# Prompt attention: the second head's probabilities divided on GpSimd between its masks, in place of ScalarE

## What is computed

```python
def fox_block(q, k, v, cq, ck, qpos, kpos):
    s = jnp.einsum('bqhd,bkhd->bhqk', q, k).astype(jnp.float32) * (HEAD_DIM ** -0.5)
    bias = jnp.swapaxes(cq, 1, 2)[..., :, None] - jnp.swapaxes(ck, 1, 2)[..., None, :]
    mask = kpos[None, :] <= qpos[:, None]
    p = jax.nn.softmax(jnp.where(mask, s + bias, -jnp.inf), axis=-1)
    return jnp.einsum('bhqk,bkhd->bqhd', p.astype(v.dtype), v)
```

## Time and profile before

| What | Value |
| --- | --- |
| time, median of 3 runs | 2518.85 us (2517.77 to 2520.33) |
| span of the profiled execution, first to last instruction | 2515.4 us |
| PE busy | 2438.8 us, 97% |
| DVE busy | 1502.0 us, 60% |
| ACT busy | 1078.2 us, 43% |
| POOL busy | 138.5 us, 6% |
| prompt attention | from 652.4 to 695.9 us of the span |
| PE busy in 665.50 to 675.32 us | 8.68 of 9.82 us |

### The profile page before, as it was taken

The page is one execution under the profiler, slowest core; times in us unless marked ns, Lnnn a source line. Parts: engine busy times, 40 slices in busy tenths (PEclk is TensorE's granted clock), DMA queues, the critical chain, the costliest instruction groups (busy, mean ns, idle before and its releaser), DMA issues. The chain is left out here.

```text
span 2515.4 us, 46249 instructions
## 1 busy us (share of the span) xinstructions
PE 2438.8 (97%) x18529; PEld 2219.3 (88%) x18529; DVE 1502.0 (60%) x2111; ACT 1078.2 (43%) x1873; POOL 138.5 (6%) x150
## 2 busy tenths in 40 slices
PE   8999999999988989999999999999999999999998
PEld 7998998899667877998999899899989779988997
DVE  7754764423546866873675687267462478735754
ACT  5542543322645654452353445245352444523542
POOL 0000001000203421000000100000010010000001
PEclk9999999999999999999999999999999999999999
DMA  4222324222480004322223332223423132322332
GB/s 134 84 86 74 84 65 152 60 75 62 151 267 20 4 13 142 85 75 88 80 84 124 119 84 75 96 73 90 136 75 97 63 102 84 92 80 75 90 105 104
DMA packets 285466, 229.41 MB, mean 91 GB/s; under 512 B 24924, under 2 KB 237046, under 8 KB 285320
## 3 DMA queue, kind: packets, MB, share of 16 engines
q1 hardware_dynamic: 285320, 227.38, 30.0%
HBM read 212.43 MB, written 14.91 MB: 90 GB/s over the span
## 5 line engine op out<-in xcount | busy, mean ns | idle before, releaser
L544 PE MATMUL ps<-row_hi,hid_hi 128*128 128x512 f32 x880 | 345.5, 393 | 0.0
L544 PE MATMUL ps<-row_hi,hid_lo 128*128 128x512 f32 x880 | 344.6, 392 | 0.0
L544 PE MATMUL ps<-row_lo,hid_hi 128*128 128x512 f32 x880 | 344.4, 391 | 0.0
L485 DVE TENSOR_TENSOR row_lo<-row_raw,row_hi 128x512 fp32r<-128x512 f32 x200 | 143.5, 731 | 265.9 <-ACT row_hi L477 265.7
L477 ACT ACTIVATE row_hi<-row_raw 128x512 fp32r<-128x512 f32 x200 | 124.1, 629 | 406.6 <-DMA row_raw<-in_ffn_w_out_dram 217.5
L544 PEld LDWEIGHTS ps<-row_lo,hid_hi 128*128 128x128 f32 x880 | 165.2, 188 | 36.9
L544 PEld LDWEIGHTS ps<-row_hi,hid_hi 128*128 128x128 f32 x880 | 165.1, 188 | 36.1
L544 PEld LDWEIGHTS ps<-row_hi,hid_lo 128*128 128x128 f32 x880 | 165.1, 188 | 36.0
L736 PE MATMUL ps<-t_hi,pair_hi 128*128 128x320 f32 x608 | 188.2, 310 | 3.0 <-DVE hid L1017 3.0
L736 PE MATMUL ps<-act_lo,pair_hi 128*128 128x320 f32 x608 | 187.9, 309 | 0.0
L736 PE MATMUL ps<-t_lo,pair_hi 128*128 128x320 f32 x608 | 187.9, 309 | 0.0
(11 more groups left out here) (453 smaller groups left out, 5688.9 us busy)
## 6 DMA issues: line engine op xcount, KB each, us to landing
pair_raw<-in_ffn_w_in_dram SPq DMA_DIRECT2D x104, 512.0 KB, 5.1
row_raw<-in_ffn_w_out_dram SPq DMA_DIRECT2D x160, 256.0 KB, 2.9
ring_raw<-in_ffn_w_in_dram SPq DMA_DIRECT2D x72, 512.0 KB, 5.2
pair_raw<-in_even_w_in_dram SPq DMA_DIRECT2D x22, 512.0 KB, 3.8
x_memory<-x SPq DMA_DIRECT2D x15, 512.0 KB, 2.6
x<-x_memory SPq DMA_DIRECT2D x15, 512.0 KB, 4.2
norm_buf<-in_norm_g_dram SPq DMA_DIRECT2D x12, 512.0 KB, 5.4
x<-in_x_prompt_dram SPq DMA_DIRECT2D x8, 512.0 KB, 4.9
```

Of the source, the lines that this page charges most:

```text
L485: dve.tensor_tensor(row_lo[n][:, :], raw, row_hi[n][:, :].bitcast(F32), ALU.subtract).then_inc(s_row_lo, 1)
L544: mm = pe.matmul(ps[:, bank, :], a[:, k, t * P:(t + 1) * P], w[n][:, :], start=(k == 0 and w is row_hi and a is left_hi), stop=(k == kt - ...
```

## The change

The second head's division leaves ACT. POOL does it with a `tensor_scalar` by the same column of reciprocals, in place on the same rows, behind the same wait for `s_rs`, and sets the same semaphore `s_np`. POOL does masks 0 and 1 first, and then by turns the division of step n and the mask of step n+2. Nothing else is changed. Later lines move: the file of the changed kernel has one line more behind this place, and ACT's lines in between have lower numbers.

```diff
@@ -1546,14 +1546,7 @@
                                    bias=nmax[:, b + h:b + h + 1], scale=-1.0,
                                    accum_out=esum[:, b + h:b + h + 1]).then_inc(s_ex, 1)
 
-            def normalised(n):
-                p, qt, kl, b = pstep(n)
-                act.wait_ge(s_rs, n + 1)
-                act.activation(prob[n % 2][1][:, 0:kl], prob[n % 2][1][:, 0:kl], ACT.Copy,
-                               scale=rsum[:, b + 1:b + 2]).then_inc(s_np, 1)
-
             exponentials(0)
-            normalised(0)
             exponentials(1)
             for n in range(PSTEPS + 1):
                 if n < PSTEPS:
@@ -1562,8 +1555,6 @@
                     if n >= 2:
                         act.wait_ge(s_o, n - 1)
                     act.activation(prob_t[n % 2][0][:, 0:kl], ps[:, 4, 0:kl], ACT.Copy).then_inc(s_pta, 1)
-                if n + 1 < PSTEPS:
-                    normalised(n + 1)
                 if n >= 1:
                     p, qt, kl, b = pstep(n - 1)
                     act.wait_ge(s_o, n)
@@ -1637,10 +1628,20 @@
                 pool.tensor_tensor(block, block, causal.rearrange("p (o c) -> p o c", o=1).broadcast_to([P, 2, P]),
                                    ALU.add).then_inc(s_mask, 1)
 
+            def normalised(n):
+                p, qt, kl, b = pstep(n)
+                pool.wait_ge(s_rs, n + 1)
+                pool.tensor_scalar(prob[n % 2][1][:, 0:kl], prob[n % 2][1][:, 0:kl], rsum[:, b + 1:b + 2], None, ALU.mult)\
+                    .then_inc(s_np, 1)
+
             pool.wait_ge(s_att_const, 16)
             pool.wait_ge(s_cr, 16 * 4)
+            mask(0)
+            mask(1)
             for n in range(PSTEPS):
-                mask(n)
+                normalised(n)
+                if n + 2 < PSTEPS:
+                    mask(n + 2)
             pool.wait_ge(s_fall, 16 * NSEQ)
             pool.tensor_copy(f_twice[:, :, 64:128], f_all).then_inc(s_f_twice, 1)
```

## The result

The change makes the kernel slower. The time after is 2531.09 us, the median of four runs (2528.63 to 2533.63), beside 2519.59 us for four runs of the kernel before. The ratio is 1.0043, with a 95% interval of 1.0031 to 1.0054: 11 us where 1.4 were forecast, and outside the range. The profiled run took 2528.63 us.

A forecast was written before the change was run, and what follows sets the result against it. A chain of waits through exponentials, DVE and PE was taken as the bound, not ACT. Late second heads, 4 x (0.20 + 0.16) = 1.4 us, gave 2518.85 + 1.4 = 2520.3 us; the range was 2517.0 to 2526.0 us.

The forecast's parts named there:

- What is added: 16 divisions on POOL, 0.78 us at 512 keys and 0.63 at 384, making PE's second-head transposes 0.20 and 0.16 us late.
- The formula around it: POOL's division ends at DVE's division end plus its own duration less 0.14 us; PE starts 0.05 us later.
- D: Duration of POOL's second-head division, put at 0.78 us at 512 keys and 0.63 at 384.
- r: Start of DVE's reciprocal in a step, from which the prediction counts the times of DVE, POOL and PE.
- sign of being wrong: The prediction would be wrong above all if DVE's division lengthened or POOL's duration fell outside 0.6 to 1.3 us.
- At 256 columns free: PE wants the second head at r + 1.66; POOL's result is ready by r + 1.19 at the latest, costing nothing.
- ACT's removal: Taking 16 divisions, 8.9 us in all, off ACT gains nothing, since DVE's division and biased scores take longer.
- The masks' place: Masks behind POOL's divisions cost nothing; DVE's 256-column division falls from 0.62 to 0.35 us, which gains nothing.
- Biased scores don't collide with POOL: DVE's biased scores, with one input in PSUM, run beside POOL's division; taken as free.
- Rival 2: DVE first, but POOL's division slower than its two-input product: over 5.0 us slower, near 2526 us, chance 0.07.
- Rival 1: POOL goes first and DVE's division ends only after POOL's: 5.2 us slower, 2524.0 us, chance 0.2.
- Rivals 3 and 4: Biased scores wait for POOL, 5.3 us slower, chance 0.04; exponentials earlier close PE's gaps, at most 4.6 us gained, chance 0.04.

## Why the prediction was wrong

**The step that failed is "What is added": POOL's division costed at 0.78 us at 512 keys and 0.63 at 384.** It is 1.56 and 1.24 us alone. I had placed it between the copy and the two-input product because it has one input like the copy. The runs show that inputs don't set it: the same division as a product of two inputs takes 1.04 us, with one input 1.56. The rows of the trace thus were no bounds. The formula around it was exact: with D = 1.56, POOL ends at r + 0.69 + 1.56 - 0.14 = r + 2.11, PE starts at r + 2.16, and r + 2.17 was measured; at 384 with 1.24, r + 1.77, and so it was. Put into the prediction's own sum, the measured durations give 4 x (0.98 + 0.77) = 7.0 us where it had 1.4. The prediction had named a POOL duration outside 0.6 to 1.3 us as its sign of being wrong, and so it came. The Trainium skill, "GPSIMD Engine Reference", section 3.1, gives 1.03 cycles per element for such a body. By this an estimate for 384 more columns is 0.33 us; the trace doesn't agree, at 1564 - 602 ns = 0.96 us, three times as much.

**"At 256 columns free" held in three groups of four.** The due time r + 1.66 counted on the next group's scores, which the last group doesn't have. There the short steps cost 0.85 us. With it the sum is 7.9 us, against 7.7 measured.

**What held.** DVE goes first and keeps its 0.49 and 0.42 us. Its 256-key division fell to 0.35 us (354 ns). ACT's removal gained nothing that the runs show: without its short divisions a middle group was still 9.82 and 9.80 us, and with all of them gone a group grew by 1.70 us for 1.76 us of lateness. The masks' place costs nothing. Biased scores don't collide with POOL: 0.55 us each with POOL's division running at 681.65 and 682.13. The last POOL copy kept nobody.

**The rivals.** Rival 2, POOL slower than its two-input product, is what happened, with a chance of 0.07 and a time near 2526 us; its size was open upwards and I gave it almost none. Rival 1, POOL first, didn't occur in the change, but it did in all sixteen steps with the product of two inputs, and in one step with the constant factor. Rivals 3 and 4 didn't occur.

**The total** has a second part that the prediction left out: the lower clock. It was 0.9924 on average against 0.9950, and what brought it there is not shown.

## What to carry to other kernels

A duration on GpSimd isn't to be interpolated between other operations: one form can cost 1.5 times another that does more. Before work is moved to an engine that looks idle, compare the time that its result has with the operation's whole duration there, and measure that first. Here, by the prediction's own terms, only a division of up to 0.58 us would have been in time at 512 keys (1.18 - 0.05 + 0.14 - 0.69), and it takes 1.56. An engine's free time counts only where the result has time to wait, as in the short steps, and the last round of a loop, which has no next round's work as a cover, has to be costed by itself.

## What the runs showed of the hardware

- `tensor_scalar` on GpSimd, f32, 128 partitions, with nothing beside it: 1.56, 1.24, 0.92 and 0.60 us at 512, 384, 256 and 128 columns. `tensor_tensor` with the factor broadcast: 1.04, 0.83, 0.61 and 0.40 us, while it holds DVE up.
- What decides who goes first is open; the start in the trace doesn't tell it. Against DVE's `tensor_scalar`, which started 0.05 to 0.07 us earlier, GpSimd's `tensor_scalar` by the column of factors came second in every step of the change. Its `tensor_tensor` with the factor broadcast, 0.04 to 0.05 us behind DVE, came first in all 16 steps. But the `tensor_tensor` that multiplies by a mask of 64 columns, repeated four times, behind DVE's `tensor_scalar` at 843.05, came second, 0.05 us behind, and so it did in the profile of the change at 851.32, 0.03 us behind (DVE 0.21 us, POOL 0.77). The `tensor_scalar` with a constant came second in 15 steps and first in one. So neither the lead in the trace nor one-input against two-input explains all of them. The Trainium skill, "SBUF — State Buffer", section "Who interferes with whom", lets whoever issues first hold the ports; by the starts in the trace the runs with the broadcast factor don't agree.
- Between a mean granted clock of 0.997 and one of 0.993 lay 8.6 us of time, in 71 runs of one and the same kernel.
